# Attention softmax: division on GpSimd, the sink as a score column, and another order of TensorE's work

## The chip, the cores and the metric

The kernel runs on one core of a Trainium2 chip. The metric is the device time of the core in microseconds (us). The engines are PE (TensorE), DVE (VectorE), ACT (ScalarE), POOL (GpSimd) and SP (SyncE, here only an issuer of DMAs).

## The reference, cut to what matters

The reference is a first block (convolution module, attention, feed-forwards with modulation) and a second block (sliding-window attention, a recurrent mixer, an attention over a memory, a feed-forward). All inputs are float32. Three attentions concern us. The sliding-window one of the second block shows the form of all of them:

```
logits = jnp.where(valid, logits + bias, -jnp.inf)          # logits already times HEAD_DIM ** -0.5
sink = sinks.reshape(...)                                    # one number for each head
m = jnp.maximum(jnp.max(logits, axis=-1, keepdims=True), sink)
e = jnp.exp(logits - m)
p = e / (jnp.sum(e, axis=-1, keepdims=True) + jnp.exp(sink - m))
out = einsum(p, v)
```

The first block's attention has 16 query heads on 4 key heads, 512 tokens in bands of 128, keys of the neighbouring bands and 256 context keys, and a sink. The second block has 6 heads with a bias by distance and a sink, and 4 heads over a memory of 256 tokens without a sink.

## The kernel before

Each engine has its own program, written out by hand, and the programs meet only at counting semaphores. An attention is an object (`Attention`) with a list of units and groups. A **unit** is the scores of one head for one band of 128 queries. A **group** is the units whose output is taken together: 4 in the first block (`ATT1`: 16 groups, 64 units, of 512 key columns in the first and last band of each key head and 640 in the two middle ones), 6 or 4 in the second (`ATT2`: 4 groups of 6, then 4 of 4, 40 units of 129 to 257 columns).

A unit passes these steps, and these names are used below:

- **S** (`scores`, L1984): PE writes the scores to one of two PSUM pairs. Each product is split into high and low parts, and masks are added as products with an identity. S of unit u waits until the exponential of unit u-2 has read its pair.
- **maximum** (L2049), a drain, and one small operation that scales and negates it and takes the smaller of it and the negated sink (L2052 in `ATT1`, L2055 in `ATT2`), on DVE.
- **exponential** (L2093) on ACT, with the sum of the row; in `ATT1` also the exponential of the sink (L2092).
- **division**: DVE adds the sink's part (L2061), takes the reciprocal (L2063), and multiplies the row in SBUF (L2066). There are three row buffers.
- **T** (`turn`, L1999): PE transposes the row in tiles of 128 into three PSUM banks, in two parts for `ATT1`.
- **copies** of the transposed parts to SBUF (`bring_out`): both by ACT in `ATT1` (L2098); in `ATT2` the units take turns between ACT and DVE (L2040).
- **V** (`values`, L2012): PE multiplies with the values, a quarter of a group's products (2 or 3 in `ATT1`) in each of four successive iterations; they use 64 of the array's columns. V0 to V3 are these quarters.
- **high and low part** of the output: ACT copies it rounded to `x_hi` (L2103), DVE subtracts (L2071). V0 of the next group waits for this subtraction, since both groups use one PSUM bank.

The iterations of each engine's loop run over u, and a row of lags says which unit each step serves: `TURN, VALUES, OUT_A, OUT_D, HIGH, LOW = 1, 2, 2, 3, 6, 7`. PE's iteration is S(u+2), T(u-1), V. ACT's is exponential(u), copies (u-2), high part of the group that ended at u-6. DVE's is maximum(u), division(u-1), its copies (u-3), low part of the group that ended at u-7.

POOL has no step in an attention. During `ATT1` it waits between two weight chunks; at the start of `ATT2` it prepares the recurrent mixer's keys (`rw_pre_pool`, L2943 and L2945).

Of the kernel before, what the change touches and what calls it, by code (L numbers as in the profile page):

```python
# [6 lines left out]
P = 128  # L7
# [8 lines left out]
HD = 64  # L16
TAPS = 31
# [77 lines left out]
def constants():  # L95
# [55 lines left out]
class Program:  # L151


    def __init__(self, nc, ctx, A):
# [112 lines left out]
        self.nsk = nxt("nsk", [16])  # L267
# [5 lines left out]
        self.p1 = nxt("p1", [3, 648])  # L273
# [3 lines left out]
        self.p2 = nxt("p2", [3, 264])  # L277
# [100 lines left out]
def build_in(nc, ctx, A, out, stop):  # L378
# [77 lines left out]
    att_p = sem("att_p")  # L456
    att_n = sem("att_n")
# [1079 lines left out]
    zero_col = M.one[:, 2:3]  # L1537

# [386 lines left out]
    class Unit:  # L1925
# [15 lines left out]
    SCALE = HD ** -0.5  # L1941
    TURN_BANK, OUT_BANK = 4, 7
    TURN, VALUES, OUT_A, OUT_D, HIGH, LOW = 1, 2, 2, 3, 6, 7

    class Attention:
# [26 lines left out]

        def turn_ps(self, j):
            return (TURN_BANK + j % 3) * 512

    def att_pe(pe, X, first=None):
# [10 lines left out]
        def turn(u):  # L1987
            x = X.units[u]
            pe.wait_ge(att_n, done(X.u0 + u + 1))
            for m, (k0, nk, _) in enumerate(x.parts):  # L1990
# [7 lines left out]
                for k in range(0, nk, P):  # L1998
                    mm = pe.transpose(M.ps[:, X.turn_ps(j) + k:X.turn_ps(j) + k + P],  # L1999
                                      X.p[:, u % 3, k0 + k:k0 + k + P], ident)  # L2000
                mm.then_inc(att_t, 1)

        def values(g, quarter):
            grp, e = X.groups[g], X.last[g]
            if quarter == 0:
# [1538 lines left out]
```

## Time and profile before

| | us |
|---|---|
| median of 3 runs | 2412.74 |
| lowest, highest | 2409.75, 2416.72 |
| the profiled execution, its own time | 2414.43 |
| its span, first to last instruction | 2412.6 |
| `ATT1` in it, first S to the first product of the output projection | 1025.5 to 1169.2 |
| `ATT2` in it, first S to the last subtraction | 1733.1 to 1798.5 |

A row of the timeline has the start, the length, the engine, the line, the operation, the names, the shapes and how many it merges; in square brackets stands the idle time before it and what ended it. PE is the matrix products, PEld the loading of their weights, which overlaps them. An f32 product of V is two records in the trace. "issue" is idle time that the profile puts down to nothing.

### The profile page before, as it was taken

The page shows a single profiled execution, that of the slowest core. Times are in us where ns is not written, and L with a number is a line of the kernel's source. Part 1 is how long each engine was busy: PE and PEld are TensorE (multiplying, and loading weights), DVE is VectorE, ACT ScalarE, POOL GpSimd, SP SyncE. Part 2 cuts the span into 40 slices and gives each one's busy share as a digit, 9 for nine tenths or more (in the row PEclk, how much of TensorE's full clock was granted, in tenths as well). Part 3 has the DMA queues.
Part 4 walks back from the last instruction along what each step waited for, and adds up shares of the span by engine and source line. Part 5 has one row for each costly group of instructions (what it writes and reads, how often), then busy time and mean ns, then how long its engine had stood idle before and what let it go on. Part 6 is the DMA issues. An engine that isn't in the chain of part 4 may idle for free.

```text
span 2412.6 us, 37223 instructions
## 1 busy us (share of the span) xinstructions
PE 2258.1 (94%) x14399; PEld 1868.9 (77%) x14399; DVE 1170.6 (49%) x2044; ACT 994.5 (41%) x1685; POOL 859.1 (36%) x449
## 2 busy tenths in 40 slices
PE   4999598999999998999989999989988889999998
PEld 3888487888888887877778888877746777878877
DVE  3699824332033325678433223458465436540541
ACT  5666544332133314588444324444353213441441
POOL 1699324223223324400244444433301113444443
PEclk8999898999999998999989999999888989999999
DMA  8778011222122221300123333332200002332332
GB/s 274 254 255 274 25 53 53 61 62 74 57 61 61 71 70 55 96 19 1 45 88 96 102 90 96 102 105 79 83 1 1 2 2 70 102 103 84 97 106 83
DMA packets 337730, 205.96 MB, mean 85 GB/s; under 512 B 5997, under 2 KB 335287, under 8 KB 337591
## 3 DMA queue, kind: packets, MB, share of 16 engines
q1 hardware_dynamic: 331915, 193.83, 26.9%
q10 hardware_dynamic: 5676, 10.24, 1.4%
q8 instruction: 93, 1.52, 0.3%
q14 instruction: 46, 0.38, 0.1%
HBM read 200.28 MB, written 2.19 MB: 84 GB/s over the span
## 4 chain that ended last, share of the span: by engine, by line
PE 72%; issue 11%; POOL 5%; DVE 5%; ACT 3%; DVEq 1%; SPq 1%; DMA 1%; ACTq 1%; POOLq 0%
PE ps L621 21%; PE ps L622 21%; PE ps L623 21%; POOL w_lo L548 2%; POOL pc L1608 2%; DVE ps L1576 1%; PE ps L894 1%; PE ps L1984 1%; PE ps L2012 1%; ACT w_hi L591 1%; DVE m L3214 1%; PE ps L3013 1%; DMA ada_x<-in_ada_w 1%; PE ps L1668 0%; SPq L772 0%
## 5 line engine op out<-in xcount | busy, mean ns | idle before, releaser
L548 POOL TENSOR_TENSOR w_lo<-raw,w_hi 128x1024 fp32r<-128x1024 f32 (+1 forms) x203 | 526.2, 2593 | 1073.4 <-ACT w_hi L591 1056.8
L621 PE MATMUL ps<-x_hi,w_hi 128*128 128x512 f32 (+1 forms) x1896 | 686.5, 362 | 35.1 <-DVE x_lo L1479 14.0
L622 PE MATMUL ps<-x_lo,w_hi 128*128 128x512 f32 (+1 forms) x1896 | 676.2, 357 | 0.0
L623 PE MATMUL ps<-x_hi,w_lo 128*128 128x512 f32 (+1 forms) x1896 | 674.9, 356 | 0.0
L591 ACT ACTIVATE w_hi<-raw 128x1024 fp32r<-128x1024 f32 (+1 forms) x251 | 280.6, 1118 | 615.8 <-PE ps L623 610.5
L621 PEld LDWEIGHTS ps<-x_hi,w_hi 128*128 128x128 f32 x1896 | 365.1, 193 | 100.0 <-issue 22.8
L622 PEld LDWEIGHTS ps<-x_lo,w_hi 128*128 128x128 f32 x1896 | 365.5, 193 | 50.0 <-issue 1.7
L623 PEld LDWEIGHTS ps<-x_hi,w_lo 128*128 128x128 f32 x1896 | 364.7, 192 | 50.5
L1858 DVE SCALAR_TENSOR_TENSOR f_a<-ps,prm,f_a 128x511 f32<-128x511 f32 (+2 forms) x176 | 116.2, 681 | 378.5 <-ACT f_b L1820 367.6
L621 PE MATMUL ps<-g_hi,w_hi 128*128 128x512 f32 (+1 forms) x704 | 256.8, 365 | 3.9 <-DVE g_lo L1867 1.7
L622 PE MATMUL ps<-g_lo,w_hi 128*128 128x512 f32 (+1 forms) x704 | 255.7, 363 | 0.0
L623 PE MATMUL ps<-g_hi,w_lo 128*128 128x512 f32 (+1 forms) x704 | 255.3, 363 | 0.0
L574 POOL TENSOR_TENSOR w_lo<-raw,w_hi 128x1024 fp32r<-128x1024 f32 x50 | 119.6, 2394 | 209.8 <-ACT w_hi L591 209.8
L1576 DVE SCALAR_TENSOR_TENSOR ps<-vp,prm,ps 128x512 f32<-128x512 f32 x320 | 169.4, 617 | 3.5 <-PE ps L956 3.5
L621 PEld LDWEIGHTS ps<-g_hi,w_hi 128*128 128x128 f32 x704 | 132.8, 189 | 26.7 <-DVE g_lo L1867 4.6
L623 PEld LDWEIGHTS ps<-g_hi,w_lo 128*128 128x128 f32 x704 | 132.7, 188 | 21.0
L622 PEld LDWEIGHTS ps<-g_lo,w_hi 128*128 128x128 f32 x704 | 132.8, 189 | 20.2
L1820 ACT ACTIVATE f_a<-ps,prm 128x512 f32<-128x512 f32 (+1 forms) x66 | 55.8, 845 | 211.0 <-PE ps L623 209.0
L621 PE MATMUL ps<-xg_hi,w_hi 128*128 128x512 f32 x352 | 137.7, 391 | 2.4 <-POOL w_lo L548 2.4
L1608 POOL TENSOR_TENSOR pc<-pc,pt 128x768 f32<-128x768 f32 x72 | 132.5, 1840 | 17.5 <-ACT pt L1597 10.6
L622 PE MATMUL ps<-xg_lo,w_hi 128*128 128x512 f32 x352 | 137.0, 389 | 0.0
L623 PE MATMUL ps<-xg_hi,w_lo 128*128 128x512 f32 x352 | 137.0, 389 | 0.0
(384 smaller groups left out, 2969.3 us busy)
## 6 DMA issues: line engine op xcount, KB each, us to landing
raw<-in_ffn_w_up SPq DMA_DIRECT2D x88, 512.0 KB, 3.8
ada_tail<-in_ada_w SPq DMA_DIRECT2D x22, 1024.0 KB, 7.4
raw<-in_ffn_w_down SPq DMA_DIRECT2D x32, 704.0 KB, 4.6
raw<-in_w_up SPq DMA_DIRECT2D x44, 512.0 KB, 3.8
ada_s<-in_ada_w SPq DMA_DIRECT2D x20, 1024.0 KB, 7.9
raw<-in_conv_w_pw SPq DMA_DIRECT2D x24, 512.0 KB, 6.3
raw<-in_w_down SPq DMA_DIRECT2D x16, 704.0 KB, 4.6
raw<-in_w_in SPq DMA_DIRECT2D x17, 512.0 KB, 3.9
```

The source lines that it names most:

```text
L548: pool.tensor_tensor(M.w_lo[:, slot, 0:K * P], M.raw[:, slot, 0:K * P], M.w_hi[:, slot, 0:K * P].bitcast(F32), ALU.subtract).then_inc(lo_r ...
L574: pool.tensor_tensor(M.w_lo[:, slot, 0:K * P], M.raw[:, slot, 0:K * P], M.w_hi[:, slot, 0:K * P].bitcast(F32), ALU.subtract).then_inc(lo_r ...
L591: act.activation(M.w_hi[:, slot, 0:K * P], M.raw[:, slot, 0:K * P], ACT.Copy).then_inc(hi_ready, 1)
L621: pe.matmul(o, wh, hi[:, k, t0:t0 + tn], start=first, stop=False)
L622: pe.matmul(o, wh, lo[:, k, t0:t0 + tn], start=False, stop=False)
L623: return pe.matmul(o, wl, hi[:, k, t0:t0 + tn], start=False, stop=last)
L894: mm = pe.matmul(M.ps[32 * q:32 * q + 32, at:at + P], M.sc32[:, k, :], weights[q // 2][:, k, q % 2 * P:(q % 2 + 1) * P], start=(k == 0), s ...
L1576: dve.scalar_tensor_tensor(out=o, in0=src, scalar=w, in1=o, op0=ALU.mult, op1=ALU.add)\
L1608: pool.tensor_tensor(acc, acc, M.pt[:, m % PT_RING, :], ALU.add).then_inc(pool_tap, 1)
L1820: ins = act.activation(dst[:, slot, 0:w], M.pair(pr, 0, w), ACT.Identity, scale=ffn_cols(b, zero_tap, t, hf, j), bias=ffn_cols(b, None, t, ...
L1858: ins = dve.scalar_tensor_tensor(out=dst[:, slot, o0:o1], in0=M.pair(pr, o0 + sh, o1 + sh), scalar=ffn_cols(b, tap, t, hf, j), in1=dst[:, ...
L1984: mm = pe.matmul(M.pair(u % 2, off, off + n), lhs, rhs, start=first, stop=True, skip_group_check=True)
```

## The change

- **Division.** DVE no longer multiplies the row. It takes the reciprocal of two units' sums in one instruction (signal `att_r`), and POOL multiplies each row with it (`att_pool`), as an operation of two steps: times the reciprocal, plus zero.
- **Maximum.** One reduction writes the maximum negated; the drain and the small operation after it go. The scale is taken into the queries' rotation tables and norms, so that the exponential has scale 1. For the keys the rotation gives it back, with two instructions of another form in each of two tiles. The second block's bias is no longer divided by the scale.
- **Sinks.** In `ATT1` the sink becomes one more column of scores, written by a product of a matrix of ones with a 2-column operand. `ATT2` had that column already. The exponential of the sink and the addition go.
- **Copies.** In `ATT1` the context part goes from ACT to DVE.
- **Order.** The lags become `TURN, OUT_A, OUT_D, VALUES, PIECES_V, HIGH, LOW = 3, 3, 4, 5, 4, 8, 9`, PE's iteration becomes V, T(u-3), S(u+2), and there are five row buffers.

```diff
-    TURN, VALUES, OUT_A, OUT_D, HIGH, LOW = 1, 2, 2, 3, 6, 7
+    TURN, OUT_A, OUT_D, VALUES, PIECES_V, HIGH, LOW = 3, 3, 4, 5, 4, 8, 9
...
-        for u in range(n_u + VALUES + 3):
+        for u in range(n_u + VALUES + PIECES_V):
+            for piece in range(PIECES_V):
+                for g in X.groups_at(u, VALUES + piece):
+                    values(g, piece)
+            if 0 <= u - TURN < n_u:
+                turn(u - TURN)
             if u + 2 < n_u:
                 scores(u + 2)
-            if 0 <= u - TURN < n_u:
-                turn(u - TURN)
-            for quarter in range(4):
-                for g in X.groups_at(u, VALUES + quarter):
-                    values(g, quarter)
...
-            dve.tensor_reduce(M.sm_max[:, b:b + 1], M.pair(u % 2, x.at, x.at + x.nk), AX.X, ALU.max)
-            dve.drain()
-            if x.sink:
-                dve.tensor_scalar(M.sm_neg[:, b:b + 1], M.sm_max[:, b:b + 1], -SCALE, x.sink[1], ALU.mult, ALU.min)\
-                    .then_inc(att_m, 1)
...
+            dve.tensor_reduce(M.sm_neg[:, b:b + 1], M.pair(u % 2, x.at, x.at + x.nk), AX.X, ALU.max, negate=True)\
+                .then_inc(att_m, 1)
...
-            p = X.p[:, u % 3, 0:x.nk]
-            dve.tensor_scalar(p, p, M.sm_rd[:, b:b + 1], None, ALU.mult).then_inc(att_n, 1)
+            b = u % 8
+            dve.wait_ge(att_p, done(X.u0 + u + 2))
+            dve.reciprocal(M.sm_rd[:, b:b + 2], M.sm_sum[:, b:b + 2]).then_inc(att_r, 1)
...
+            if u % 2 == 0 and 0 <= u - 2 < n_u:
+                inverse(u - 2)
...
-            if x.sink:
-                act.activation(M.sm_e[:, b:b + 1], M.sm_neg[:, b:b + 1], ACT.Exp, scale=1.0, bias=x.sink[0])
...
+    def att_pool(pool, X):
+        for u, x in enumerate(X.units):
+            pool.wait_ge(att_r, done((X.u0 + u) // 2 + 1))
+            p = X.slot(u)[:, 0:x.n_keys]
+            pool.tensor_scalar(p, p, M.sm_rd[:, u % 8:u % 8 + 1], zero_col, ALU.mult, ALU.add).then_inc(att_n, 1)
...
-                    scores += [(SEQ, CTX, q, M.k_hi[:, g, SEQ:TOK], True), (SEQ, CTX, q, M.k_lo[:, g, SEQ:TOK], False)]
+                    scores += [(SEQ, CTX, q, M.k_hi[:, g, SEQ:TOK], True), (SEQ, CTX, q, M.k_lo[:, g, SEQ:TOK], False),
+                               (TOK, 2, M.fr[:, P:2 * P], M.sk1[:, h, :], True)]
...
-                    heads.append(Unit(scores, nk, [(0, nb, "A"), (nb, CTX, "A")], place, at,
-                                      (M.sinks[:, h:h + 1], M.nsk[:, h:h + 1])))
+                    heads.append(Unit(scores, nk, [(0, nb, "A"), (nb, CTX, "D")], place, at))
...
                 rw_pre_pool(pool)
+                att_pool(pool, ATT2)
                 V_S.after(pool, "abc2")
```

The first place is PE in `ATT1`, from the last quarter of one group's V to the first of the next. `pt` is the transposed rows, `vt` the values, `p` the row, `kb` the identity for transposes, `k_hi`, `k_lo`, `q`, `fr` and `sk` the operands of S. Before:

```order
L2012 MATMUL ps<-pt_117,vt 64x256 x2
L1984 MATMUL ps<-k_hi,q_108 128x384 [waits att_p]
L1984 MATMUL ps<-k_lo,q_108 128x384
L1984 MATMUL ps<-fr 128x128 x2
L1984 MATMUL ps<-k_hi,q_108 128x256
L1984 MATMUL ps<-k_lo,q_108 128x256
L1999 MATMUL ps<-kb,p_116 128x128 [waits att_ea,att_n]
L1999 MATMUL ps<-kb,p_116 128x128 x2
L1999 MATMUL ps<-kb,p_116 128x128 [waits att_ea]
L1999 MATMUL ps<-kb,p_116 128x128
L2012 MATMUL ps<-pt_117,vt 64x256 [waits att_x,att_ed,att_ea]
```

And now:

```order
L2021 MATMUL ps<-pt_117,vt 64x256 x2
L2008 MATMUL ps<-kb,p_4_112 128x128 [waits att_ed,att_n]
L2008 MATMUL ps<-kb,p_4_112 128x128 x2
L2008 MATMUL ps<-kb,p_4_112 128x128 [waits att_ea]
L2008 MATMUL ps<-kb,p_4_112 128x128
L1993 MATMUL ps<-k_hi,q_106 128x256 [waits att_p]
L1993 MATMUL ps<-k_lo,q_106 128x256
L1993 MATMUL ps<-fr 128x128
L1993 MATMUL ps<-k_hi,q_106 128x256
L1993 MATMUL ps<-k_lo,q_106 128x256
L1993 MATMUL ps<-sk_110,fr 128x2
L2021 MATMUL ps<-pt_117,vt 64x256 [waits att_x,att_ed,att_ea]
```

S and T have changed places between V and V, and S ends with the sink's product.

The second place is ACT around the high part of a group's output in `ATT1` (`x_hi`; `pt` are the copies of transposed parts, `p` the exponentials). Before:

```order
L2098 ACTIVATE pt_117<-ps 128x3x128 [waits att_o,att_t]
L2098 ACTIVATE pt_117<-ps 128x2x128 [waits att_o,att_t]
L2103 ACTIVATE x_hi<-ps 128x2x128 [waits att_o]
L2092 ACTIVATE sm_e<-sm_neg,sinks 128x1 [waits att_t,att_m]
L2093 ACTIVATE p_116,sm_sum<-ps,sm_neg 128x512
```

And now:

```order
L2090 ACTIVATE p_116,sm_sum<-ps,sm_neg 128x513 [waits att_t,att_m]
L2095 ACTIVATE pt_117<-ps 128x2x128 [waits att_o,att_t]
L2100 ACTIVATE x_hi<-ps 128x2x128 [waits att_o]
L2090 ACTIVATE p_116,sm_sum<-ps,sm_neg 128x513 [waits att_t,att_m]
L2095 ACTIVATE pt_117<-ps 128x2x128 [waits att_o,att_t]
```

One copy of two is left ahead of the high part; by the lags it is that of the unit ended + 5, where before it was of ended + 4.

## Rows read from the trace of the kernel before

**Rows 1.** The page: busy time and share of each engine over the span.

```profile
PE 2258.1 (94%) x14399; PEld 1868.9 (77%) x14399; DVE 1170.6 (49%) x2044; ACT 994.5 (41%) x1685; POOL 859.1 (36%) x449
```

**Rows 2.** Windows in ATT1: stretch, length, busy of each engine, clock, DMA share, GB/s.

```profile
1060.00:1077.00 17.00, 17.00 (x120) 11.80 (x118) 14.58 (x43) 14.29 (x46) 0.00 (x0) 1.00 0.01 2
...
1025.50:1169.20 143.70, 137.15 (x940) 99.40 (x940) 113.68 (x336) 116.77 (x339) 2.38 (x1) 0.98 0.03 9
```

**Rows 3.** Timeline, weight loads of one iteration of PE in ATT1, 512 columns.

```profile
1060.77 0.19 PEld L1984 LDWEIGHTS ps<-k_hi,q 128*128 128x128 f32 x1 [0.39 <-ACTq L2095]
...
1061.36 0.46 PEld L1999 LDWEIGHTS ps<-kb,p 128*128 128x128 f32 x4
...
1061.99 0.62 PEld L2012 LDWEIGHTS ps<-pt,vt 128*64 128x64 f32 x6 [0.17 <-issue]
...
1063.00 0.19 PEld L1984 LDWEIGHTS ps<-k_hi,q 128*128 128x128 f32 x1 [0.39 <-issue]
```

**Rows 4.** Waits, 1034 to 1162: us in total, times, longest.

```profile
PEld ps L1984 <- issue: 18.5, 48, 0.4
...
PEld ps L1984 <- ACTq L2095: 4.7, 11, 0.6
```

**Rows 5.** Timeline at the end of ATT1, where T follows V.

```profile
1163.07 0.65 PE L2012 MATMUL ps<-pt,vt 128*64 128x256 f32 x4
1163.65 0.42 PEld L1999 LDWEIGHTS ps<-kb,p 128*128 128x128 f32 x4 [0.39 <-issue]
...
1164.13 0.66 ACT L2098 ACTIVATE pt<-ps 128x256 f32<-128x256 f32 x2 [0.57 <-PE ps L1999]
1164.24 0.62 PEld L2012 LDWEIGHTS ps<-pt,vt 128*64 128x64 f32 x6 [0.17 <-issue]
```

**Rows 6.** Timeline in ATT2, the sink's product between another one and T.

```profile
1746.73 0.28 PE L1984 MATMUL ps<-bias_lo,fr 128*128 128x256 f32 x1
...
1746.85 0.16 PE L1984 MATMUL ps<-sk,fr 128*128 128x2 f32 x1
1746.86 0.20 PEld L1999 LDWEIGHTS ps<-kb,p 128*128 128x128 f32 x2
```

**Rows 7.** Timeline in ATT1, from V3 of one group to V0 of the next.

```profile
1066.02 1.08 PE L2012 MATMUL ps<-pt,vt 128*64 128x256 f32 x6
...
1067.13 0.39 ACT L2103 ACTIVATE x_hi<-ps 128x256 fp32r<-128x256 f32 x1 [0.45 <-PE ps L2012]
...
1067.55 0.42 DVE L2071 TENSOR_TENSOR x_lo<-ps,x_hi 128x256 fp32r<-128x256 f32 x1
...
1068.24 0.20 PEld L2012 LDWEIGHTS ps<-pt,vt 128*64 128x64 f32 x4 [0.17 <-issue]
```

**Rows 8.** Groups of POOL's instructions by form: busy us, mean ns, idle before.

```profile
L1608 POOL TENSOR_TENSOR pc<-pc,pt 128x768 f32<-128x768 f32 x72 | 132.5, 1840 | 17.5 <-ACT pt L1597 10.6
...
L1718 POOL TENSOR_SCALAR diag<-kb,prm 128x128 f32<-128x128 f32 x8 | 4.8, 602 | 0.1
...
L2943 POOL TENSOR_SCALAR behind<-pj,prm,one 128x512 f32<-128x512 f32 x3 | 2.3, 766 | 0.4 <-DVE pj L2623 0.4
```

**Rows 9.** Windows at the start of ATT1, columns as in rows 2.

```profile
1030.00:1032.00 2.00, 0.00 (x0) 0.00 (x0) 0.00 (x0) 1.99 (x4) 0.00 (x0) 0.85 0.59 176
...
1034.00:1036.00 2.00, 1.84 (x8) 1.44 (x8) 1.77 (x6) 1.34 (x5) 0.00 (x0) 0.50 0.00 0
```

**Rows 10.** Waits, 1725 to 1800, around ATT2.

```profile
ACT p L2093 <- DVE sm_neg L2055: 16.9, 24, 2.7
...
PEld ps L1984 <- ACTq L2095: 7.4, 12, 0.9
```

**Rows 11.** Timeline in ATT2: POOL's last preparation, a maximum and its exponential.

```profile
1737.72 1.04 POOL L2945 TENSOR_TENSOR behind<-behind 128x512 f32<-128x512 f32 x1
...
1755.56 0.43 DVE L2049 TENSOR_REDUCE sm_max<-ps 128x1 f32<-128x257 f32 x1 [0.37 <-PE ps L1984]
...
1756.25 0.48 ACT L2093 ACTIVATE p<-ps,sm_neg 128x257 f32<-128x257 f32 x1 [0.96 <-DVE sm_neg L2055]
```

More of the change, by code:

```diff
@@ L272, in __init__ @@
         o = self.mod_rows_at
-        self.p1 = nxt("p1", [3, 648])
+        p1 = nxt("p1", [3, 648])
+        self.p1 = [p1[:, i, :] for i in range(3)] + [t[:, :] for t in p1_more]
         self.pt1 = nxt("pt1", [2, 5 * 4 * P])
@@ L276, in __init__ @@
         o = r_s
-        self.p2 = nxt("p2", [3, 264])
+        p2 = nxt("p2", [3, 264])
+        self.p2 = [p2[:, i, :] for i in range(3)] + [at(f"p2_{3 + i}", r_raw + i * w + behind_8, [264])[:, :] for i in (0, 1)]
         self.pt2 = nxt("pt2", [2, 2 * 6 * P])
@@ L1537, in build_in @@
     zero_col = M.one[:, 2:3]
+    eps_q_col = M.one[:, 4:5]
     VLAT, VCTX = PAD, SEQ + 3 * PAD
@@ L1925, in build_in, with __init__ @@
     class Unit:
-        def __init__(self, scores, nk, parts, place, at=0, sink=None):
-            self.scores, self.nk, self.at, self.sink = scores, nk, at, sink
+        def __init__(self, scores, nk, parts, place, at=0):
+            self.scores, self.nk, self.at = scores, nk, at
             self.parts, self.place = parts, place
+            self.n_keys = sum(n for _, n, _ in parts)
     class Group:
@@ L2086, in exps @@
         def exps(u):
-            x, b = X.units[u], u % 4
+            x, b = X.units[u], u % 8
             act.wait_ge(att_m, done(X.u0 + u + 1))
-            if u >= 3:
-                act.wait_ge(att_t, done(X.t0 + X.turned[u - 3]))
-            if x.sink:
-                act.activation(M.sm_e[:, b:b + 1], M.sm_neg[:, b:b + 1], ACT.Exp, scale=1.0, bias=x.sink[0])
-            act.activation(X.p[:, u % 3, 0:x.nk], M.pair(u % 2, x.at, x.at + x.nk), ACT.Exp, scale=SCALE,
+            if u >= len(X.p):
+                act.wait_ge(att_t, done(X.t0 + X.turned[u - len(X.p)]))
+            act.activation(X.slot(u)[:, 0:x.nk], M.pair(u % 2, x.at, x.at + x.nk), ACT.Exp, scale=1.0,
                            bias=M.sm_neg[:, b:b + 1], accum_out=M.sm_sum[:, b:b + 1])
@@ L2173, in qkv_act @@
                 act.wait_ge(s_kf, 16)
+                act.activation(M.sk1[:, :, :], M.sinks[:, 0:16].unsqueeze(2).to_broadcast([P, 16, 2]), ACT.Copy,
+                               scale=1.0 / HD)
                 act.activation(M.fr[:, 0:2 * P], M.kb[:, 0:2 * P], ACT.Copy)
@@ L2603, in w_in_act @@
                 for n in range(3):
[L2604 to L2605 removed]
+                    ins = act.activation(M.bias[:, 2 * n:2 * n + 2, :], halves(odd(BIAS_BANK[n])), ACT.Copy)
                 S_S.mark(ins, "bhi")
@@ L3379, in _ @@
                 rw_pool(pool)
+                low_stream(pool, name, 2, 8)
+                continue
+            if name == "wo":
+                low_stream(pool, name, 0, 2)
+                att_pool(pool, ATT1)
                 low_stream(pool, name, 2, 8)
```

81 lines of the change are left out of this document (43 added, 38 removed).

## The prediction

> **What bounds the kernel now.** I read the page first: PE is busy for 94% of the span, the others for 36 to 49% [rows 1]. So the question for each edit is whether it takes time from PE or gives PE time. `ATT1` and `ATT2` are the only stages that the change touches to any extent, so I looked at the windows next. `ATT1` takes 143.70 us, and in its steady part PE is busy for 17.00 of 17.00 us at full clock, while DVE has 14.58 and ACT 14.29 [rows 2]. DVE and ACT are near, but behind.
>
> The timeline shows that PE is really working. In one iteration S loads at 1060.77, T at 1061.36, V at 1061.99, and the next S at 1063.00 [rows 3]. So S costs 0.59 us, T 0.63 with the 0.17 gap behind it, and V 1.01. This V had three products, of which two run side by side in the halves of the array. A V of two products costs 0.58, from 1163.07 to 1163.65 [rows 5]. Iterations are therefore 1.80 or 2.23 us. The gaps of 0.17 and 0.39 in the weight loads are not waits for another engine: they come back with the same length at every change between the 128-column products and the 64-column ones of V [rows 3, 5], and "issue" makes up 18.5 us of them. The 4.7 us put down to ACT are 11 gaps [rows 4], and 11 times 0.39 is 4.3: about 0.4 us of true waiting in 128 us. In `ATT1` a faster ACT or DVE cannot give anything back. `ATT2` is different: there the exponential waits 16.9 us for the maximum and PE 7.4 us for ACT [rows 10], so a shorter chain can pay.
>
> **The change part by part.**
>
> *Division, maximum, copies.* The nearest row for POOL's two-step operation is 0.766 us for 512 columns [rows 8], so 0.77 us for a unit of 512 and by proportion 0.96 for 640. A PE iteration is 1.80 or more, so POOL is busy for half of it. T now comes three iterations behind, 5.4 us or more, and the pair of divisions takes at most 1.9, so it is hidden; with the price of a two-input operation, 1840 ns for 768 columns, or 1.53 us for 640 [rows 8], it still is. DVE and ACT become lighter. In `ATT1` PE covers all of this, and I cost it at nothing. The rotation's other form for two key tiles and the sink's preparation lie beside weight loads of the `qkv` stage: nothing.
>
> *The sink's product, and the order.* The 64 units of `ATT1` each get one more product. In `ATT2` it starts 0.12 us after the one before it (1746.73 to 1746.85) though it moves 2 columns only, and the load for T follows as before [rows 6]. Cyclically the order was S, T, V and is now S, V, T. V to T costs the same gap as V to S, 0.39 [rows 3, 5]. T without its gap takes 0.42 behind V (1163.65 to 1164.24, less 0.17, rows 5) and took 0.46 behind S (0.63 less 0.17, rows 3). T to S I take without a gap, as S to T is. S to V no row of before shows. Its bounds: no gap, and the 0.17 of T to V. I take 0.11: the change of mode is the same, but the last product before it is 0.16 long where others are 0.28 [rows 6], so less is left in the array. The new iteration is 0.58 + 0.42 + 0.59 + 0.12 + 0.11 = 1.82 against 1.80: **+0.02 for a unit, +1.3 us** for 64. Its bounds are 1.71 and 1.88, that is -5.8 and +5.1 us.
>
> Two rules bear on these terms. The trace has 0.12 us for the 2-column product. The Trainium skill ("TensorE: Matmul & The Clock Gate", in "Wait — 56ns, not 53.3ns?") gives a floor of about 25 ns between starts of very small products; by that figure 64 sinks would be an estimated 1.6 us and not 7.7, but its own section "LDWEIGHTS (loading the stationary operand)" charges a load by its 128 columns, and the trace agrees with that one. For S to V, "TensorEngine Tiling (Array Packing)" says under "Key Properties" that changing the tiling mode drains the array. By it the gap appears whichever step stands before V, which speaks against the lower bound; the rows on both sides of V agree.
>
> *The high part.* This is what I find the trace to say against the change. V0 of a group waits for the low part of the group before. Before, ACT took the high part 0.03 us after V3 ended (1066.02 + 1.08, then 1067.13), DVE was done at 1067.97, and PE came to V0 at 1068.07 without its gap [rows 7]: clear by 0.10 us. Now T of the unit ended + 5 stands behind V3 on PE, and its copy stands ahead of the high part on ACT. Measured from the end of V3 (1163.72 in rows 5), such a copy starts at +0.41. Two copies take 0.66 where one takes 0.38, so ACT is free for the high part at +0.69; with 0.39, then 0.03 and 0.42 for the low part, and 0.03 again, V0 may start at +1.56. PE is there at -0.07 + 0.42 + 0.59 + 0.12 + 0.11 = +1.17. It waits 0.39 us. For 640 columns both sides grow. There are 15 boundaries, and the last lies in the run-out, where PE waits for the low part already: 14 x 0.4 = **+5.6 us**. Bounds: 0, if the copy is out of the way earlier than I think, and 14 x 0.6 = 8.4.
>
> *Start and end of ATT1.* Before the first exponential PE stands idle, and it then works at clock 0.50 [rows 9], the lower of two levels (1.2 GHz). Now T begins two iterations later, so PE has less to do in this phase and may stay at that level longer; but nothing is lost of the work, it is only done later, and ACT's extra exponential is gone. I take 0, with bounds -2 and +3 us (3 us at half clock is 1.5 us of work).
>
> *ATT2.* The chain from maximum to exponential is 0.69 us (1755.56 to 1756.25) and becomes 0.43 plus a signal's 0.03 [rows 11]: 0.23 us less. PE's 12 waits for ACT [rows 10] could give 2.8 us. Against it: POOL is in its preparation until 1738.76 [rows 11], so the first division and T wait for it, about 0.5 us of PE's time; four groups of four units get the wait at V0, 4 x 0.4; and DVE and ACT meet in new orders. I take 0, with bounds -3 and +3.
>
> **The sum.** 1.3 + 5.6 + 0 + 0 = **+6.9 us**. The profiled execution took 2414.43 us, its span 2412.6; the median is 2412.74, 1.7 below it. On the median the forecast is 2419.6 us. A measurement of this kernel can tell about 0.3%, 7.2 us, from no change, so the forecast stands just at that line.
>
> **The rivals.**
>
> - *PE pays in full.* Nothing of S to V's gap is saved, 1.88 for an iteration: +5.1, and with it +5.6 and about +1 for the cold start: +11.7, 2424. For it: every gap at V in the trace has a fixed length. Against: the short last product.
> - *The change to V is free behind the short product.* Then -5.8, and PE comes to V0 0.11 earlier, so the waits grow to 14 x 0.5 = 7: +1.2, 2414. For it: no row shows S to V.
> - *Faster.* DVE and ACT set the pace in a way that the records hide: they are at 84 to 86% in the steady part [rows 2], and PE's ends are modelled. If both the gap is free (-5.8) and the wait at V0 does not arise because ACT, lighter by a small exponential and a copy for each unit, takes the high part early, and `ATT2` gains its 2.8 us, it is -8.6: 2404. It decides at a wait at V0 under 0.1 us. Against: ACT takes its steps in order, and the copy cannot start before its transposes.
> - *POOL becomes the bound.* The one-step form has 602 ns for 128 columns [rows 8], 2.4 us for 512, above 1.80. If the two-step operation ran at such a price on these rows, 64 x 0.6 to 1.0 = +38 to 64 us. Against: the same form with the same kind of operands has 766 ns for 512. It decides at 1.8 us for a division.
>
> **How the numbers follow.** Forecast, +2 to +9: 0.42. PE pays in full, +9 to +14: 0.24. Free change, -4 to +2: 0.17. Faster: 0.10. POOL or a longer cold phase, above +14: 0.07. The range leaves out most of the last two and reaches from -3 to +15: 2410 to 2428. Slower by over 7.2 us: 0.24 + 0.07 and a third of the forecast's 0.42, 0.45. Faster by as much: 0.09, nearly all of that rival. Between: 0.46.
>
> **What would show it.** In the profile after: an iteration of 512 columns with two products of V at 1.80 to 1.84 us; a gap at S to V near 0.1; "V waits for the low part" (L2070) in `ATT1` with about 14 waits of 0.4 us; POOL's divisions at 0.77 us for 512 and no engine waiting for them; `ATT1` at 149 to 152 us against 143.7; `ATT2` within 3 us of 65. The forecast is wrong if the waits at V0 are missing, if S to V costs 0.17 or nothing, if POOL's operation is slower while DVE works, or if the clock stays at the lower level past the first ten units.

## The result

| | us |
|---|---|
| median after, 20 runs (lowest, highest) | 2416.32 (2414.31, 2427.81) |
| median before, 20 runs beside them (lowest, highest) | 2411.57 (2408.45, 2417.44) |
| ratio after to before, 95% interval | 1.0024, 1.0015 to 1.0033 |
| forecast, range | 2419.6, 2410 to 2428 |

The change makes the kernel slower by 4.7 us or 0.2%, under the 0.3% that I took as the line of "no change". The direction and the range were right, and so was the mechanism that I gave most weight, the wait at V0. Three terms of the sum were off by 2 to 5 us each and cancelled in large part.

The profiled execution after took 2414.42 us with a span of 2412.6, the very figures of before (2414.43 and 2412.6). That is a coincidence, as the stretches show. The recurrent mixer stands behind `ATT2`; it is cut at its first product with 64x64 weights (L2977 before, L2993 after), and "the mixer from there" runs to the first product of the feed-forward.

| stretch, us | before | before again | after | after again |
|---|---|---|---|---|
| start to first S of `ATT1` | 1025.5 | 1028.6 | 1025.7 | 1026.0 |
| `ATT1` | 143.7 | 143.7 | 149.7 | 150.2 |
| to the first S of `ATT2` | 563.8 | 564.1 | 564.3 | 563.4 |
| `ATT2` | 65.4 | 64.9 | 64.0 | 65.5 |
| to the mixer's first 64x64 product | 31.1 | 31.0 | 31.4 | 31.1 |
| the mixer from there | 156.6 | 156.6 | 151.5 | 157.0 |
| feed-forward to the end | 426.4 | 426.4 | 426.0 | 426.3 |
| span | 2412.6 | 2415.3 | 2412.6 | 2419.4 |

`ATT1` costs 6.0 to 6.5 us more, and repeats within 0.5. What hid it in the first profile after is the mixer, which the change does not touch. These are the windows of "the mixer from there" in the two executions of the changed kernel, the columns as in rows 2:

```profile
1835.10:1986.60 151.50, 129.12 (x2242) 111.55 (x2242) 68.71 (x164) 36.93 (x94) 27.48 (x42) 0.88 0.01 2
```

```profile
1836.10:1993.10 157.00, 133.09 (x2242) 115.05 (x2242) 68.65 (x164) 36.77 (x94) 27.56 (x42) 0.86 0.01 2
```

The same 2242 products run at a mean clock of 0.88 in one and 0.86 in the other, and take 5.5 us more: PE is busy for 4.0 us longer and pauses for 1.5 longer. Why the clock stood lower in one execution of the same kernel, no run shows. Over the ten profiles of ten variants and the four of the two kernels, this stage took between 151.1 us (mean clock 0.89) and 161.6 (0.82), though not in strict order of the clock.

Because of this the medians depend on which clock the runs happened to get. Over the runs whose clock is listed, by the mean granted clock of the run (median, number of runs):

| clock | before | after |
|---|---|---|
| 0.965 | 2410.2 (13) | 2416.4 (6) |
| 0.962 | 2415.4 (2) | 2421.9 (4) |
| 0.960 | 2417.9 (8) | 2426.7 (2) |

In these three rows the difference is 6 to 9 us, against 4.7 between the medians. The clocks that are left out give 8.4 (0.959) and 6.5 (0.964), and 4.5 to 5.2 where one kernel has a single run (0.961, 0.966, 0.967). The groups are small, and a run's clock is itself a mean over a program that has changed, so I take this as consistent with the 6 us that the stretches show and not as a measurement of its own.

**The profile after.** The first lines of the page, for [rows 1]:

```profile
PE 2251.2 (93%) x14463; PEld 1874.4 (78%) x14463; DVE 1120.3 (46%) x1784; ACT 959.4 (40%) x1558; POOL 932.6 (39%) x554
```

DVE is busy for 50 us less and ACT for 35, POOL for 74 more, and PE has its 64 products more. The work did move. For [rows 2], the same 17 us of the steady part, and all of `ATT1`:

```profile
1060.00:1077.00 17.00, 16.24 (x123) 12.45 (x122) 10.31 (x22) 9.40 (x26) 6.02 (x9) 1.00 0.00 1
...
1025.72:1175.42 149.70, 136.88 (x1005) 107.41 (x1005) 83.11 (x176) 82.53 (x211) 53.90 (x65) 0.97 0.03 8
```

DVE has gone from 14.6 to 10.3 and ACT from 14.3 to 9.4 of 17 us, and PE, which was busy for 17.00, now has holes. The engine that bounds the stage has lost time while the two behind it were relieved. Who made the holes is in the summary of the line of the low part (instructions, durations, first and last start, then who waited, us in total and times):

```profile
L2070 DVE TENSOR_TENSOR x_lo<-ps,x_hi x16: 423/425/426, 1054.1 to 1174.9; 128x256 fp32r<-128x256 f32 x16
...
  PE ps L2021: 7.9, 15
```

The kernel before has 1.0 us and one wait there:

```profile
L2071 DVE TENSOR_TENSOR x_lo<-ps,x_hi x16: 417/422/425, 1051.2 to 1168.7; 128x256 fp32r<-128x256 f32 x16
...
  PE ps L2012: 1.0, 1
```

The timeline of the changed kernel from V3 of a group to V0 of the next, for [rows 7]:

```profile
1060.72 1.08 PE L2021 MATMUL ps<-pt,vt 128*64 128x256 f32 x6
...
1062.20 0.38 ACT L2095 ACTIVATE pt<-ps 128x256 f32<-128x256 f32 x1 [1.03 <-PE ps L2008]
...
1062.48 0.38 ACT L2100 ACTIVATE x_hi<-ps 128x256 fp32r<-128x256 f32 x1
...
1062.89 0.42 DVE L2070 TENSOR_TENSOR x_lo<-ps,x_hi 128x256 fp32r<-128x256 f32 x1
...
1063.46 0.65 PE L2021 MATMUL ps<-pt,vt 128*64 128x256 f32 x4 [0.49 <-DVE x_lo L2070]
```

V3 ended at 1061.80. ACT sits idle for 1.03 us until T is done, copies, and only then, at 1062.48, takes the high part. The low part follows at once, and V0 after 0.49 us of waiting.

An iteration of PE with two products of V, the weight loads, for [rows 3, 5]:

```profile
1066.62 0.19 PEld L1993 LDWEIGHTS ps<-k_hi,q 128*128 128x128 f32 x1
...
1067.20 0.19 PEld L1993 LDWEIGHTS ps<-sk,fr 128*128 128x128 f32 x1
...
1067.41 0.20 PEld L2021 LDWEIGHTS ps<-pt,vt 128*64 128x64 f32 x4
...
1068.00 0.42 PEld L2008 LDWEIGHTS ps<-kb,p 128*128 128x128 f32 x4 [0.39 <-issue]
...
1068.38 0.19 PEld L1993 LDWEIGHTS ps<-k_hi,q 128*128 128x128 f32 x1
```

S with the sink's product and all of the gap takes 0.79, V 0.59, T 0.38: 1.76 us.

### The profile page after: what moved, and what is told of

It is laid out like the page before. It is cut to its first block, busy times and chain, and to the rows that moved or that the text cites. A ratio compares the mean times of both kernels' runs of the same rounds, so it can differ in the third digit from the quotient of the medians.

```text
span 2412.6 us, 36779 instructions
## 1 busy us (share of the span) xinstructions
PE 2251.2 (93%) x14463; PEld 1874.4 (78%) x14463; DVE 1120.3 (46%) x1784; ACT 959.4 (40%) x1558; POOL 932.6 (39%) x554
## 4 chain that ended last, share of the span: by engine, by line
PE 77%; DVE 10%; issue 4%; POOL 3%; ACT 3%; DVEq 1%; ACTq 1%; SPq 1%; DMA 1%; POOLq 0%
PE ps L626 21%; PE ps L627 21%; PE ps L628 21%; DVE ps L1582 5%; PE ps L2021 3%; PE ps L1993 2%; PE ps L2008 2%; POOL w_lo L553 1%; ACT w_hi L596 1%; DVE m L3230 1%; PE ps L3029 1%; PE ps L3016 1%; DMA ada_x<-in_ada_w 1%; PE ps L1674 0%; SPq L777 0%
```

## The experiments

All times of `ATT1` below are from each variant's own profile, first S to the first product of the output projection. "Ten groups" is the time from the fourth low part to the fourteenth; it lies in the steady part, at full clock, and repeats: 83.55 and 83.54 us in the two executions of before, 85.86 and 85.87 in those of after.

| variant | ten groups | `ATT1` | `ATT2` | waits of V for the low part |
|---|---|---|---|---|
| before | 83.5 | 143.7 | 65.4, 64.9 | 1.0 |
| after | 85.9 | 149.7, 150.2 | 64.0, 65.5 | 7.9 |
| `e2_hl_first` | 81.0 | 142.4 | 60.5 | 1.5 |
| `e4_no_sink` | 85.7 | 148.1 | 65.5 | 7.9 |
| `e5_two_sinks` | 89.1 | 155.2 | 63.9 | 6.4 |
| `e7_onestep` | 85.9 | 150.4 | 66.1 | 7.9 |
| `e6_div_dve` | 95.1 | 165.5 | 65.0 | 20.8 |
| `e6b_div_hl` | 81.1 | 143.3 | 61.8 | 1.6 |
| `e9_pieces2` | 81.6 | 141.6 | 66.1 | 0 |
| `e10_pieces3` | 82.6 | 143.1 | 61.1 | 0 |
| `e3_stv` | 120.9 | 207.9 | 84.7 | 1.4 |
| `e3b_stv` | 97.8 | 167.6 | 69.4 | 1.0 |

### Both kernels again

> The changed kernel again, to see what of its profile repeats. My theory: the stretches that the change touches repeat, so ATT1 (first S to the first product of the output projection) is within 0.5 us of 149.7 and ATT2 within 0.5 us of 64.0, with PE's waits for the low part near 7.9 us; what differs from execution to execution is the recurrent mixer behind ATT2, where the clock falls to its lower level in short pieces, by some 5 us. Ratio to the kernel before 1.002 to 1.003. Rival: the 5 to 6 us that the profiled execution had regained by 1980 us belong to the change; then this execution regains them too, in the same place.

> The kernel before again, for what of its profile repeats. My theory: ATT1 within 0.3 us of 143.7, ten groups of it (fourth to fourteenth low part) in 83.5, ATT2 within 2 us of 65.4; the recurrent mixer's stage lies anywhere between 151 and 157 us by the time that it spends at half clock, and makes up nearly all that two executions of one kernel differ by. Rival: ATT2 or the stages around it differ as much.

2422.73 us in 4 runs, at clocks of 0.959 to 0.962, for the changed kernel. The kernel before, run beside it, had 2411.61, so the ratio was 1.0051 (1.0034 to 1.0068) and not the 1.002 to 1.003 that I expected. This interval does not meet the 1.0015 to 1.0033 of the result: what differs from one set of runs to the next is not in either interval, and "4.7 us" is no firmer than "some 5 to 11". A later set gave the kernel before 2415.02 in 8 runs. The stretches are in the table at the top. `ATT1` repeats within 0.5 us and the mixer does not, for the changed kernel (151.5 and 157.0); `ATT2` of the changed kernel differed by 1.5, more than expected. The rival, that the 5 us regained behind `ATT2` belong to the change, falls: the second execution did not regain them. Both profiles of before gave 156.6, so its mixer's spread is not seen in the profiles, only in the run times, and the stretch ahead of `ATT1`, which I had left out, moved by 3.1.

### The low part, taken early

```diff
             if u < n_u:
                 exps(u)
+            for g in X.groups_at(u, HIGH):
+                high_part(g)
             if 0 <= u - OUT_A < n_u:
                 bring_out(act, copy, X, u - OUT_A, "A", att_t, att_ea)
-            for g in X.groups_at(u, HIGH):
-                high_part(g)
```

and the same in DVE's loop, `low(g)` ahead of its copy.

> One change against the changed kernel: ACT takes a group's high part ahead of the copy of the iteration, and DVE the low part ahead of its copy, so that neither waits for a transpose that stands behind V3 on PE. My theory (V0 waits because the high part stands behind such a copy): from the end of V3 the chain is 0.03 + 0.39 + 0.03 + 0.42 + 0.03 = 0.90 us, and PE comes to V0 at about 1.15, so the waits for the low part go from 7.9 us to under 1.5, ATT1 from 149.7 to about 144, the whole by 5 to 6 us against the changed kernel. Rival (PE pays for the sink's product and the gap, or for the start, and the wait only covers other idle time): the waits for the low part vanish, others come in their place, and ATT1 stays at 148 or more.

2410.76 us (10 runs), ratio to before 0.9996 (0.9986 to 1.0006). That is 5.6 below the 2416.3 of the result and 12.0 below the 2422.7 of the changed kernel run beside it. The low part's line in this variant:

```profile
L2070 DVE TENSOR_TENSOR x_lo<-ps,x_hi x16: 423/425/425, 1052.9 to 1167.3; 128x256 fp32r<-128x256 f32 x16
...
  PE ps L2021: 1.5, 2
```

The two waits that are left lie in the run-out, the iterations behind the last S. In the timeline the order has turned round:

```profile
1060.79 0.38 ACT L2100 ACTIVATE x_hi<-ps 128x256 fp32r<-128x256 f32 x1 [0.66 <-PE ps L2021]
...
1061.16 0.38 ACT L2095 ACTIVATE pt<-ps 128x256 f32<-128x256 f32 x1
...
1061.21 0.42 DVE L2070 TENSOR_TENSOR x_lo<-ps,x_hi 128x256 fp32r<-128x256 f32 x1 [0.73 <-ACT x_hi L2100]
...
1061.87 0.65 PE L2021 MATMUL ps<-pt,vt 128*64 128x256 f32 x4
```

ACT waits for V3 and not for T, the low part ends at 1061.63, and V0 starts at its own time. No other instruction is changed, and nothing took the place of the wait: `ATT1` lost 7.3 us and `ATT2` 3.5 to 5.0. This settles the cause of the loss in `ATT1`. The high part and the low part were moved together; that it is the high part's place on ACT which counted here is read from the timeline above, where the low part followed it at once. The variant also gives the rest of the change on its own: `ATT1` is 1.3 us *shorter* than before.

### The sink's product

`e4_no_sink` leaves the product and the column out, so that the sinks have no part in this softmax; `e5_two_sinks` issues a second such product into columns that nobody reads.

```diff
-                nk = CTX + nb + 1
+                nk = CTX + nb
...
-                               (TOK, 2, M.fr[:, P:2 * P], M.sk1[:, h, :], True)]
```

```diff
+                               (TOK + 2, 2, M.fr[:, P:2 * P], M.sk1[:, h, :], True),
                                (TOK, 2, M.fr[:, P:2 * P], M.sk1[:, h, :], True)]
```

> This kernel leaves out the sinks' column in ATT1: 64 products less, and rows of 512 and 640 columns, so the sinks have no part in the first block's softmax. Two theories of what the 2-column product costs. (a) The gap between S and V hides behind it: without it the last product is a 256-column one, the gap is 0.17 us, and S to V is 0.59 + 0.17 = 0.76 against 0.78 now: the product is nearly free, ATT1 falls by 1 to 2 us. (b) The product costs its 0.12 us and the gap is what it is: S to V 0.66, 64 x 0.12 = 7.7 less, of which 1.8 come back as a longer wait at V0: ATT1 about 144. I hold (a).

> One change against the changed kernel: each unit of ATT1 gets a second 2-column product, into two columns that nobody reads, just ahead of the sink's. Theories of the price of such a product once the gap to V is already covered by the first: (a) a product is charged by its weight load, 0.12 us as in rows 6: 64 x 0.12 = 7.7, less up to 1.8 that V0 then waits less, so ATT1 goes from 149.7 to 150.2 up to 155.5 to 158. (b) A floor of some tens of ns: 1.6 us or less, ATT1 stays under 152.

2422.75 us without the product (4 runs), 2430.84 with two (3 runs). Weight loads from the last product of the scores to V, without the sink's product:

```profile
1087.87 0.19 PEld L1993 LDWEIGHTS ps<-k_lo,q 128*128 128x128 f32 x1
1088.20 0.62 PEld L2021 LDWEIGHTS ps<-pt,vt 128*64 128x64 f32 x6
```

In the changed kernel, with one:

```profile
1086.37 0.19 PEld L1993 LDWEIGHTS ps<-k_lo,q 128*128 128x128 f32 x1
1086.49 0.19 PEld L1993 LDWEIGHTS ps<-sk,fr 128*128 128x128 f32 x1
1086.70 0.20 PEld L2021 LDWEIGHTS ps<-pt,vt 128*64 128x64 f32 x4
```

And with two:

```profile
1088.77 0.19 PEld L1993 LDWEIGHTS ps<-k_lo,q 128*128 128x128 f32 x1
1088.89 0.31 PEld L1993 LDWEIGHTS ps<-sk,fr 128*128 128x128 f32 x2
1089.22 0.20 PEld L2021 LDWEIGHTS ps<-pt,vt 128*64 128x64 f32 x4
```

The distance from `k_lo`'s load to V's is 0.33 us without the product, 0.33 with one and 0.45 with two. So the change from S to V takes its 0.33 us whether a small product stands in it or not, and the first sink is free; the second costs 0.12. Ten groups say the same: 85.7 without, 85.9 with, 89.1 with two. `ATT1` with two is 155.2 us, 0.3 under the range that I had for a price of 0.12. A regular group grew by 0.32 us, roughly four products of 0.12 less 0.12 that V0 then waits less. Without the sink `ATT1` is 1.6 to 2.1 us shorter, of which the ten groups show only 0.2; the rest lies ahead of the fourth low part, where the clock rises earlier (see the start of `ATT1` below). The 25 ns for a very small product, which the Trainium skill gives in "TensorE: Matmul & The Clock Gate" ("Wait — 56ns, not 53.3ns?"), would have made the second sink an estimated 1.6 us in all; the trace has 0.12 us for each, as it had in [rows 6].

### PE's old order

```diff
         for u in range(n_u + VALUES + PIECES_V):
+            if u + 2 < n_u:
+                scores(u + 2)
+            if 0 <= u - TURN < n_u:
+                turn(u - TURN)
             for piece in range(PIECES_V):
                 for g in X.groups_at(u, VALUES + piece):
                     values(g, piece)
-            if 0 <= u - TURN < n_u:
-                turn(u - TURN)
-            if u + 2 < n_u:
-                scores(u + 2)
```

> One change against the changed kernel: PE's iteration is S(u+2), T(u-3), V again, as in the kernel before; the sinks' products, the division on POOL and the other lags stay. My theory: the wait at V0 goes (T stands ahead of V3 again), -6 us; but the last product before V is a transpose and not the 2-column one, so the gap of 0.17 us comes back and the sink's product is paid beside it: iteration 0.59 + 0.12 + 0.46 + 0.17 + 0.58 = 1.92 us against 1.78 now, 0.14 x 64 = +9. ATT1 about 152 us, total +2 to +4 against the changed kernel. Rival (the order by itself costs or saves nothing in the steady iteration, all of the loss is the wait at V0): ATT1 about 144.

2496.88 us, ratio 1.0353 (1.0336 to 1.0370), `ATT1` at 207.9 us. The two theories missed it by 56 and 64 us. Waits of this variant between 1044 and 1165 us:

```profile
ACT pt L2095 <- PE ps L2008: 51.5, 30, 2.7
...
PEld ps L1993 <- ACTq L2092: 43.0, 38, 2.2
PE ps L1993 <- ACTq L2092: 25.4, 31, 1.7
ACT pt L2095 <- PE ps L2021: 22.3, 9, 2.8
```

PE waits for exponentials and ACT waits for PE. ACT's iteration is exponential(u), copy(u-3); the copy needs T(u-3), which now stands behind S(u+2), and S(u+2) waits for exponential(u). Exponential, S, T, copy and the next exponential stand in one row. The last line is a second such wait: the first copy of a group also waits for V3 of the group two back, whose buffer it takes, and in that iteration V3 now stands behind S and T. I then moved the copy by one iteration.

```diff
-    TURN, OUT_A, OUT_D, VALUES, PIECES_V, HIGH, LOW = 3, 3, 4, 5, 4, 8, 9
+    TURN, OUT_A, OUT_D, VALUES, PIECES_V, HIGH, LOW = 3, 4, 4, 5, 4, 8, 9
```

> Against the changed kernel: PE's iteration is S(u+2), T(u-3), V, and ACT's copy comes one iteration later (OUT_A = 4), so that no exponential stands behind a transpose that stands behind its own S, which is what I hold to have cost e3_stv its 80 us. The theory (the 2-column product costs PE nothing where it stands against V, and its 0.12 us where it doesn't; the gap of about 0.2 ahead of V is there whatever stands before it): S 0.71, T 0.63, V 0.58 = 1.92 us for an iteration against 1.79, so ten groups take 40 x 0.13 = 5.2 us more than the 81.0 of e2_hl_first, 86.2, without waits for the low part; ATT1 about 149 to 151. Rival (the order costs nothing by itself): ten groups in 81 to 82 us and ATT1 at 143. If the rest of e3_stv's loss has another cause, ATT1 stays above 160.

`ATT1` came down from 207.9 to 167.6 us (2439.0 in 2 runs), so that loop was a good part of it, but not to the 150 that I expected. Its copies wait for T only 5.9 us in all now, but ACT waits for V3 in the high part:

```profile
ACT x_hi L2100 <- PE ps L2021: 26.4, 11, 2.9
```

With V last in PE's iteration, V3 of the group ended at u-8 comes behind S and T, ACT waits for it in iteration u, and exponential(u+1) stands behind that wait. The two variants therefore say little of what the order of S, T and V costs PE in itself, and that question stays open. They do say that this order and these lags belong together: the old order under the new lags costs 18 to 58 us in `ATT1`.

### The division

`e6_div_dve` gives the division back to DVE, two rows behind each pair of reciprocals, with the low part behind them as in the changed kernel; `e6b_div_hl` does the same on top of `e2_hl_first`, with the low part ahead.

```diff
             dve.reciprocal(M.sm_rd[:, b:b + 2], M.sm_sum[:, b:b + 2]).then_inc(att_r, 1)
+            dve.drain()
+            for n in (u, u + 1):
+                p = X.slot(n)[:, 0:X.units[n].n_keys]
+                dve.tensor_scalar(p, p, M.sm_rd[:, n % 8:n % 8 + 1], None, ALU.mult).then_inc(att_n, 1)
...
-                att_pool(pool, ATT2)
...
-                att_pool(pool, ATT1)
```

> One change against the changed kernel: the division is DVE's again, two rows behind each pair of reciprocals, and POOL has no step in the attentions. My theory (POOL's division was hidden, DVE's would be too, PE sets the pace of ATT1): ATT1 within 1.5 us of the changed kernel's 149.7 to 150.2, and ATT2 up to 3 us longer. Rival (DVE is the hidden pace-maker, and taking the row from it is what makes the change bearable): ATT1 longer by 3 us or more, with PE or ACT waiting for DVE.

> Against e2_hl_first: the division is DVE's, in ATT1 and ATT2. The theory (DVE has room in ATT1, and in e6_div_dve it was only the low part, queued behind two divisions, that made V0 wait 1.4 us a group): with the low part ahead of copy and divisions, ten groups of ATT1 take 81 to 82.5 us as in e2_hl_first and ATT1 142.4 to 145; moving the division to POOL then brings ATT1 nothing that an order of DVE's steps doesn't. Rival (DVE is the pace-maker with the division on it): ten groups 85 us or more, with PE or ACT waiting for DVE all the way.

`e6_div_dve` took 2438.26 us and 165.5 in `ATT1`. My number for it was wrong by 14 us, and on the words of the expectation the rival had won. But the profile does not show a busy DVE (63.8 of 88 us between 1077 and 1165). It shows the same wait as before, only longer:

```profile
1086.28 1.01 DVE L2069 TENSOR_SCALAR p<-p,sm_rd 128x640 f32<-128x640 f32 x2
...
1087.21 0.42 DVE L2074 TENSOR_TENSOR x_lo<-ps,x_hi 128x256 fp32r<-128x256 f32 x1
...
1087.77 0.65 PE L2021 MATMUL ps<-pt,vt 128*64 128x256 f32 x4 [1.31 <-DVE x_lo L2074]
```

The high part was ready at 1086.23; two divisions of 0.5 us stood ahead of the low part. `e6b_div_hl` takes that away and is the clean test: ten groups in 81.1 us against 81.0 with POOL, 2411.19 us in all (ratio to before 0.9987, 0.9973 to 1.0002). Moving the division to POOL brings nothing in the steady part of `ATT1` that the order of DVE's steps doesn't. All of `ATT1` is 143.3 against 142.4, and nearly all of that 0.9 lies ahead of the fourth low part; `ATT2` is 61.8 against 60.5, no more apart than two executions of one kernel were.

```diff
-            pool.tensor_scalar(p, p, M.sm_rd[:, u % 8:u % 8 + 1], zero_col, ALU.mult, ALU.add).then_inc(att_n, 1)
+            pool.tensor_scalar(p, p, M.sm_rd[:, u % 8:u % 8 + 1], None, ALU.mult).then_inc(att_n, 1)
```

> One change against the changed kernel: POOL's division has one step (times the reciprocal) and not two. Theory (a), my rival of POOL as the bound: the one-step form costs what L1718 shows, 602 ns for 128 columns, so 2.4 us for 512 and 3.0 for 640; POOL then sets the pace of ATT1, 64 x 2.7 = 173 us and more, total +25 us and over. Theory (b): on these rows it costs the same 0.76 us as the two-step form, and nothing moves. L1718 has few instructions and other operands; I hold (a).

POOL's division by form, in the changed kernel and then in this variant (count, busy us, mean ns of one):

```profile
L2114 POOL TENSOR_SCALAR p<-p,sm_rd,one 128x640 f32<-128x640 f32 x32 | 27.7, 876 | 39.4 <-DVE sm_rd L2065 39.4
L2114 POOL TENSOR_SCALAR p<-p,sm_rd,one 128x512 f32<-128x512 f32 x32 | 24.3, 768 | 48.6 <-DVE sm_rd L2065 48.6
...
L2114 POOL TENSOR_SCALAR p<-p,sm_rd,one 128x128 f32<-128x128 f32 x6 | 2.6, 448 | 1.9 <-DVE sm_rd L2065 1.9
```

```profile
L2114 POOL TENSOR_SCALAR p<-p,sm_rd 128x640 f32<-128x640 f32 x32 | 59.9, 1884 | 9.6 <-DVE sm_rd L2065 9.5
L2114 POOL TENSOR_SCALAR p<-p,sm_rd 128x512 f32<-128x512 f32 x32 | 49.6, 1563 | 23.1 <-DVE sm_rd L2065 23.1
...
L2114 POOL TENSOR_SCALAR p<-p,sm_rd 128x128 f32<-128x128 f32 x6 | 3.5, 601 | 1.5 <-DVE sm_rd L2065 1.5
```

The variant took 2424.8 us (3 runs). Neither theory holds. The one-step form costs twice the two-step form at 512 columns. For 128 columns it takes 601 ns, as in [rows 8] (602): that row was right, and taking it by proportion to 512 was the error. By the forms shown, an instruction costs an estimated 0.28 us and 2.5 ns for a column with one step, 0.34 us and 0.84 ns for a column with two. At 1.6 and 1.9 us it is still shorter than an iteration of PE, so ten groups take 85.9 us as before, and PE does not notice. Had POOL been the bound at the 2.4 us that I worked with, it would have.

### Fewer changes to V

`e9_pieces2` takes V in two pieces, `e10_pieces3` in three, the latter on top of `e2_hl_first`.

```diff
-    TURN, OUT_A, OUT_D, VALUES, PIECES_V, HIGH, LOW = 3, 3, 4, 5, 4, 8, 9
+    TURN, OUT_A, OUT_D, VALUES, PIECES_V, HIGH, LOW = 3, 3, 4, 5, 2, 6, 7
```

```diff
-    TURN, OUT_A, OUT_D, VALUES, PIECES_V, HIGH, LOW = 3, 3, 4, 5, 4, 8, 9
+    TURN, OUT_A, OUT_D, VALUES, PIECES_V, HIGH, LOW = 3, 3, 4, 5, 3, 7, 8
```

> One change against the changed kernel: a group's V stands in two pieces in two successive iterations, not in four in four, and the high and low part are taken two iterations earlier (6 and 7 for 8 and 9). The theory of fixed gaps (0.39 us behind V whatever follows it, and about 0.07 left of the gap ahead of V): half of the changes between 128 and 64 columns go, 32 x 0.46 = 14.7 us less in ATT1, and the waits at V0 go too, -6.5: ATT1 about 129 us, if ACT and DVE keep up with an average iteration of 1.8 us. The total falls by 20 us and more with ATT2, below both kernels. Rival (the gaps are not lost time: PE's records are modelled and ACT and DVE are the real pace): ATT1 falls by no more than the 6 us of the waits at V0, to 143 or more, and PE waits for ACT or DVE instead.

> Against e2_hl_first: a group's V in three pieces, high and low part at 7 and 8. In e9_pieces2 the two iterations without V took 1.48 us, and PE waited 0.2 us in them for the exponential: the chain S, maximum, exponential sets a floor there, so ten groups came to 81.6 us and not less. The theory: with one such iteration in four, a group saves one pair of gaps (0.39 and about 0.09, against 0.2 of waiting for ACT) and V0 waits for nothing: ten groups in 78 to 80.5 us, ATT1 139.5 to 142, the whole 1 to 4 us below e2_hl_first, and below the kernel before by 0.1 to 0.2%. Rival (V in fewer and longer pieces only moves the wait to the exponential): ten groups in 81 to 82 us, nothing gained.

`e9_pieces2`: 2417.01 us (10 runs), ratio 1.0015 (1.0003 to 1.0027); `ATT1` at 141.6 us where I expected 129, and ten groups in 81.6. `e10_pieces3`: 2412.18 (12 runs), ratio 0.9988 (0.9975 to 1.0001); ten groups in 82.6, worse than with four pieces. PE's timeline in `e9_pieces2`:

```profile
1087.83 0.39 PE L1993 MATMUL ps<-k_hi,q 128*128 128x256 f32 x1
...
1089.25 0.39 PE L1993 MATMUL ps<-k_hi,q 128*128 128x256 f32 x1
...
1090.04 1.51 PE L2021 MATMUL ps<-pt,vt 128*64 128x256 f32 x10
1091.48 0.77 PE L2008 MATMUL ps<-kb,p 128*128 128x128 f32 x5
```

and in `e10_pieces3`, a V of three products and one of four (x6 and x8):

```profile
1088.71 1.08 PE L2021 MATMUL ps<-pt,vt 128*64 128x256 f32 x6
1089.72 0.77 PE L2008 MATMUL ps<-kb,p 128*128 128x128 f32 x5
...
1091.01 1.08 PE L2021 MATMUL ps<-pt,vt 128*64 128x256 f32 x8
1092.03 0.76 PE L2008 MATMUL ps<-kb,p 128*128 128x128 f32 x5
```

From its start to T, a V of two products takes 0.58 us, of three 1.01, of four 1.02, of five 1.44. That is 0.15 + 0.43 for each *pair*, an odd product paying as a pair. So the 0.39 in front of T's load is not all lost time: by this fit most of it is the last pair still at work, and one change fewer saves an estimated 0.15 behind V and about 0.09 ahead of it (0.21 us from the sink's load to V's, where a load behind the scores' other products comes after 0.12). Two pieces save some 0.5 us for a group; against that, the two iterations without V take 1.42 to 1.48 us, in which PE waits 0.2 each for the exponential. Three pieces split the 8 products of the end bands into 2, 3 and 3, 2.60 us where four pieces of 2 take 2.32. The theory of a fixed gap of 0.39 was mine and is wrong; the rival named the right place, the exponential, for half of it.

## Why the prediction was right, point by point

**What bounds the kernel.** Right. ACT and DVE were relieved by 5 and 4 us of 17 and `ATT1` got nothing for it; `e6b_div_hl` shows the same from the other side.

**Division, maximum, copies at nothing.** Right for the price of POOL (0.768 us measured, 0.766 taken; for 640 columns 0.876 where I took 0.96, again by proportion) and for being hidden. The list of waits does put 13 gaps ahead of T down to POOL, 5.0 us, but none is longer than the 0.4 of the other gaps there, and with POOL's operation twice as long (`e7_onestep`) ten groups take the same 85.9 us.

**The iteration, +0.02 us a unit and +1.3 in all.** Wrong in sign. I put it together as 1.82; measured it is 1.76. T of four tiles takes 0.38 behind V and not 0.42, and S with sink and gap 0.79, not 0.82: the gap behind the sink's product is 0.09, about the 0.11 that I chose. Ten groups of `e2_hl_first` against before give -0.064 us a unit (81.0 against 83.5 us), an estimated -4.1 for 64. The measured value lies between my forecast and the rival "the change to V is free", nearer to the rival (1.71).

**The high part, 14 x 0.4 = +5.6 us.** The mechanism is right in each step, and `e2_hl_first` proves it. The size is 7.3 us, 0.49 for a regular group. ACT took the high part 0.68 us after V3, where I had worked out 0.69. V0's first weights were then loaded 0.12 behind the low part where I had taken 0.03, and PE came 0.07 earlier because its iteration was shorter. A wait and the iteration ahead of it are not two independent terms: what PE saved on the way to V0 it waited there, as the rival had said.

**Start and end of `ATT1`, 0.** Too low, near the upper of the bounds of -2 and +3. From the first S to the fourth low part `e2_hl_first` takes 1.5 us more than before, and behind the fourteenth 0.2 less. The 24 units in these two stretches should have saved 1.5 by the steady -0.064 each, so the start costs an estimated 2.8 us. A part of it is the clock. After, in the window from 1038 to 1040 us:

```profile
1038.00:1040.00 2.00, 2.00 (x10) 2.00 (x10) 0.85 (x4) 1.00 (x3) 1.18 (x2) 0.50 0.00 0
```

The kernel before had a clock of 0.94 there, and `e2_hl_first` 0.50 like the changed kernel. PE stays some 3 us longer at 1.2 GHz, with 10 products in the window where before had 13; at half speed that is 1.5 us. That T begins two iterations later and leaves PE more idle time in front is the reason that I named. No run tested it, and one speaks against it as the whole reason: `e4_no_sink`, where T begins 11.1 us behind the first S, against 11.4 in the changed kernel and 8.9 before.

```profile
1038.00:1040.00 2.00, 1.82 (x15) 1.58 (x13) 1.91 (x5) 1.64 (x5) 0.57 (x1) 1.00 0.00 0
```

Its clock is 1.00 there, and 0.79 from 1036 to 1038, where the changed kernel has 0.69 as late as 1040 to 1042. Its first S came 1.4 us earlier, which leaves some 3 us by which its clock rises sooner. What sets that moment stays open.

**`ATT2`, 0 with -3 to +3.** Right: 64.0 and 65.5 against 65.4 and 64.9. That nothing was gained is again the order of the high and low part: with them ahead of the copies `ATT2` takes 60.5 us.

**The sum.** By the stretches it was +6.0 to +6.5 in `ATT1` and between -1.4 and +0.6 in `ATT2`, +4.6 to +7.1, against +6.9. In `ATT1` the terms came out as -4.1 for the iteration, +7.3 for the wait and +2.8 for the start, +6.0 together. So the iteration was taken too dear by 5.4 us, and the wait and the start too cheap by 4.5 together. That +6.9 lies so near to the +6.0 is luck; the sign and the cause, the wait at V0, are not. Between the medians it is +4.7.

**The rivals.** "PE pays in full" falls with the gap of 0.09. "POOL becomes the bound" falls with 0.768 us. "Faster" had its first two conditions wrong: the gap is not free, and ACT, lighter as it is, still could not take the high part early, because it takes its steps in order.

**A version that beats both.** `e2_hl_first`, `e6b_div_hl` and `e10_pieces3` are below the kernel before in their medians, by 0.04 to 0.13%, and the interval of each includes no difference. By the stretches `e2_hl_first` takes about 6 us less than before in `ATT1` and `ATT2` together; of that the run times show 0.9 (2.3 to 4.4 where runs of the same clock, 0.962 to 0.964, are set side by side), and the spread of the mixer is too wide to say where the rest is. Splitting V by whole pairs (10 products as 2, 2, 2 and 4, and not as 2, 3, 2 and 3) was not tried; by the prices above, 3 x 0.58 + 1.02 against 2 x 0.58 + 2 x 1.01, it is an estimated 0.4 us for each of the eight groups of 640 columns.

## What to carry to other kernels

When an engine takes its steps in a fixed order, look at what stands ahead of the step that the bounding engine waits for, and at what that one waits for in its turn; relieving the engine did not help here, and exchanging two of its steps, on ACT and on DVE, gave 7.3 us of `ATT1`. Moving a step on the bounding engine moves every wait that is tied to its place, so lags on the other engines have to be worked out anew. And a total that agrees with a forecast to the microsecond, or two profiles with equal spans, prove little where one stage varies by 5 us: compare the stretches that the change touches.

## What the runs showed of the hardware

- A 2-column product between the last 128-column product and the first of V costs PE nothing (0.33 us with or without it); a second one costs 0.12 us.
- A V of n pairs of 256-column products in the two halves of the array takes 0.15 + 0.43 n us until T's first load (0.58, 1.02; 1.44 for five products), and an odd product costs a whole pair (1.01 us for three). So of the 0.39 us that the weight loads stand idle ahead of T, an estimated 0.15 is the price of the change.
- POOL's multiplication by a column of scalars takes 601, 1563 and 1884 ns for 128, 512 and 640 columns in its one-step form, and 448, 768 and 876 ns with a second step that adds zero.
- One stage, the recurrent mixer, took 151.1 to 161.6 us with the same products, at mean clocks of 0.89 to 0.82.
